# Attention in pairs of heads: the work of two pairs written out as one sequence for each engine, and V split in halves

## The reference

```python
z = einsum('bthd,bshd->bhts', q, k) * HEAD_DIM ** -0.5 + bias
log_beta = log_sigmoid(z)
log_rest = where(k_pos < q_pos, log_sigmoid(-z), 0)
after = cumsum(log_rest, axis=3, reverse=True) - log_rest
a = where(k_pos < q_pos, exp(log_beta + after), 0)
out = einsum('bhts,bshd->bthd', a, v)
```

## Time and profile before

| | us |
|---|---|
| median of 3 runs | 2902.86 (2899.84 to 2904.23) |
| profiled execution | 2905.36, its span 2903.5 |
| attention stage, 1190 to 2010 us of the span | 820.0, PE busy 713.8, DVE 556.1, ACT 494.8 |
| before it, 600 to 1190 | 590.0, PE busy 584.4 |
| after it, 2010 to 2903 | 893.0, PE busy 871.4 |
| granted TensorE clock over the span | 0.960 |

### The profile page before, as it was taken

The page is one execution under the profiler, slowest core; times in us unless marked ns, Lnnn a source line. Parts: engine busy times, 40 slices in busy tenths (PEclk is TensorE's granted clock), DMA queues, the critical chain, the costliest instruction groups (busy, mean ns, idle before and its releaser), DMA issues.

```text
span 2903.5 us, 42452 instructions
## 1 busy us (share of the span) xinstructions
PE 2739.0 (94%) x16785; PEld 2601.4 (90%) x16785; DVE 1328.3 (46%) x1335; ACT 766.3 (26%) x1088; POOL 1007.3 (35%) x534
## 2 busy tenths in 40 slices
PE   7999999999999999989989988977999999999997
PEld 6989999999999999877777777756999999999997
DVE  5243543333333336567657656774343333333335
ACT  5122110000000002556656656663110000000003
POOL 4542476676767761000000000011153343333340
PEclk9999999999999999989989989977999999999998
DMA  3111133333333334222221122223211111111111
GB/s 111 51 31 37 44 116 109 110 109 110 118 113 115 110 113 162 80 72 67 68 76 61 57 78 63 69 80 110 67 58 51 45 44 45 45 51 44 44 37 60
DMA packets 247794, 220.18 MB, mean 76 GB/s; under 512 B 12842, under 2 KB 211298, under 8 KB 247586
## 3 DMA queue, kind: packets, MB, share of 16 engines
q1 hardware_dynamic: 229090, 206.75, 22.7%
q10 hardware_dynamic: 18496, 10.49, 1.2%
HBM read 162.42 MB, written 54.77 MB: 75 GB/s over the span
## 4 chain that ended last, share of the span: by engine, by line
PE 85%; DVE 6%; ACT 4%; issue 3%; ACTq 0%; DMA 0%; SPq 0%; DVEq 0%
PE ps L770 48%; PE ps L899 17%; PE aux L1029 8%; PE ps L936 3%; PE ps L981 2%; PE ps L966 2%; PE ps L954 2%; ACT zb L1312 1%; DVE scratch L1507 1%; PE aux L1000 1%; DVE sp L1637 1%; DVE a_part L1663 1%; PE aux L1035 1%; DVE zb L1670 1%; ACT zb L1323 0%
## 5 line engine op out<-in xcount | busy, mean ns | idle before, releaser
L652 POOL TENSOR_TENSOR w_hi<-w_raw,ones_col 128x1024 fp32r<-128x1024 f32 x140 | 271.0, 1936 | 825.6 <-PE ps L770 540.8
L659 POOL TENSOR_TENSOR w_lo<-w_raw,w_hi 128x1024 fp32r<-128x1024 f32 x156 | 436.1, 2796 | 12.2
L770 PE MATMUL ps<-near_hi,w_hi 128*128 128x352 f32 x1632 | 357.3, 327 | 16.3 <-DVE near_lo L1494 12.9
L770 PE MATMUL ps<-near_lo,w_hi 128*128 128x352 f32 x1632 | 354.2, 325 | 0.0
L770 PE MATMUL ps<-near_hi,w_lo 128*128 128x352 f32 x1632 | 352.5, 324 | 0.0
L726 POOL TENSOR_TENSOR in_lo<-o_back,in_hi 128x1056 fp32r<-128x1056 f32 x7 | 17.2, 2450 | 854.2 <-ACT in_hi L1173 854.2
L770 PEld LDWEIGHTS ps<-near_hi,w_hi 128*128 128x128 f32 x1632 | 278.8, 190 | 20.5 <-issue 11.6
L770 PE MATMUL ps<-in_hi,w_hi 128*128 128x352 f32 x1320 | 286.9, 325 | 3.7 <-issue 3.7
L1621 DVE TENSOR_TENSOR h<-h,ps 128x1056 f32<-128x1056 f32 x160 | 200.2, 1251 | 188.2 <-PE ps L899 188.2
L770 PE MATMUL ps<-in_lo,w_hi 128*128 128x352 f32 x1320 | 285.5, 324 | 0.0
L770 PE MATMUL ps<-in_hi,w_lo 128*128 128x352 f32 x1320 | 284.3, 323 | 0.0
(11 more groups left out here) (229 smaller groups left out, 4457.3 us busy)
## 6 DMA issues: line engine op xcount, KB each, us to landing
w_raw<-in_w_gate_dram SPq DMA_DIRECT2D x44, 512.0 KB, 3.9
w_raw<-in_w_up_dram SPq DMA_DIRECT2D x44, 512.0 KB, 3.9
w_raw<-in_w_down_dram SPq DMA_DIRECT2D x44, 512.0 KB, 3.8
kept_hi<-pre_hi SPq DMA_DIRECT2D x64, 256.0 KB, 2.1
kept_lo<-pre_lo SPq DMA_DIRECT2D x64, 256.0 KB, 2.6
w_hi<-kept_hi SPq DMA_DIRECT2D x32, 512.0 KB, 3.6
w_lo<-kept_lo SPq DMA_DIRECT2D x32, 512.0 KB, 4.5
w_raw<-in_a_w_in_dram SPq DMA_DIRECT2D x16, 512.0 KB, 4.0
```

Of the source, the lines that this page charges most:

```text
L652: gp.tensor_tensor(hi, raw, one, ALU.mult).then_inc(w_hi_done, 1)
L659: gp.tensor_tensor(lo, raw, as32(hi), ALU.subtract).then_inc(w_ready, 1)
L770: last = mm(out[:, c, 0:CH], w[:, ks], x[:, k, c * CH:c * CH + CH], start=(k == 0 and n == 0), stop=(k == KT - 1 and n == 2))
```

## The change

The loop over steps and its tables go. For each of PE, ACT and DVE `pair` now lists every item of a pair by name, in one written order, which begins with what is left over of the pair before (`past`: steps 9 to 11 of it), then the pair's own items (`now`), with the next pair's projections among them (`more`). A last call with `past` alone ends the stage. Items keep their operations and shapes. In detail:

- `softplus_split` becomes `softplus_high` and `softplus_low`, which can be placed apart; the DVE items for the sample are functions of their own, and `q_block` is no longer first in the pair.
- V's split is in two halves of 4 key blocks. `v_high(p, 1)` waits for only the first four `values` of the pair before; `values` of step 4 waits for the other half.
- `chunk_evicted` of Q and V waits for the K or Q split that reads the same part of `staged`.
- SP's and POOL's queues are unchanged.

The diff, cut:

```diff
-X1 = {0: ("c", 0), 1: ("c", 1), 2: ("k", 0), 3: ("c", 2), 4: ("c", 3), 5: ("c", 4), 6: ("c", 5), 7: ("c", 6),
-      8: ("c", 7), 9: ("c", 8), 10: ("v", 1)}
-X2 = {0: ("p", 0), 1: ("p", 1), 2: ("k", 1), 3: ("p", 2), 4: ("k", 2), 5: ("p", 3), 8: ("v", 0), 11: ("v", 2)}
...
                 pe.wait_ge(a_split, NS * p + s + 1)
-                if s == 0:
-                    pe.wait_ge(v_ready, p + 1)
+                if s in (0, TB // P):
+                    pe.wait_ge(v_ready, 2 * p + (1 if s == 0 else 2))
...
-            def pair(p, c, more=True):
-                for s in range(NS + (0 if more else 2)):
-                    if s < NS:
-                        scores(p, c, s)
-                    if s in X1 and (more or X1[s][0] == "p"):
-                        x_turn(p, c, X1[s], more)
-                    at = lagging(p, c, s, 1)
-                    if at is not None:
-                        take_later(*at)
-                    if s == S_OUT:
-                        sample_turned(p, c)
-                    if s in X2 and (more or X2[s][0] == "p"):
-                        x_turn(p, c, X2[s], more)
-                    sample(p, c, s)
-                    if s == S_VALUES:
-                        sample_values(p, c)
-                    for lag, work in ((2, values), (1, carry)):
-                        at = lagging(p, c, s, lag)
-                        if at is not None:
-                            work(*at)
+            def pair(p, c, past=True, now=True, more=True):
+                q, o = p - 1, 1 - c
+                if now:
+                    scores(p, c, 0)
+                if past:
+                    values(q, o, 9)
+                if more:
+                    x_turn(p, c, ("c", 0), more)
+                if past:
+                    carry(q, o, 10)
+                if now:
+                    scores(p, c, 1)
+                    x_turn(p, c, ("p", 0), more)
+                if past:
+                    take_later(q, o, 11)
+                    values(q, o, 10)
+                if more:
+                    x_turn(p, c, ("c", 1), more)
+                if now:
+                    take_later(p, c, 0)
+                if past:
+                    values(q, o, 11)
+                if now:
+                    scores(p, c, 2)
+                    sample_start(p, c)
+                if more:
+                    x_turn(p, c, ("k", 0), more)
+                if now:
+                    carry(p, c, 0)
+                    scores(p, c, 3)
+                    x_turn(p, c, ("p", 1), more)
+                    take_later(p, c, 1)
+                    sample_scores(p, c, 0)
...
+                    x_turn(p, c, ("c", 8), more)
+                if now:
+                    take_later(p, c, 8)
+                    values(p, c, 7)
+                    scores(p, c, 10)
+                    carry(p, c, 8)
+                    sample_later(p, c)
+                    take_later(p, c, 9)
+                    scores(p, c, 11)
+                if more:
+                    x_turn(p, c, ("v", 1), more)
+                if now:
+                    values(p, c, 8)
+                    carry(p, c, 9)
+                    sample_values(p, c)
+                if more:
+                    x_turn(p, c, ("v", 2), more)
+                if now:
+                    take_later(p, c, 10)
+                    sample_turned(p, c)
...
+            pair(PAIRS, 0, now=False, more=False)
...
-            def v_high(p):
+            def v_high(p, half):
+
                 if not isinstance(p, int) or p > 0:
-                    act.wait_ge(pv_done, NS * p)
+                    act.wait_ge(pv_done, NS * p - (NS - 4 if half else 0))
                 act.wait_ge(aux_out, X_ATT + NA * p)
-                nc.scalar.copy(v_part[:, :, 0:4:3, :], v_row[:, 0:RT, :].rearrange("p c (e d) -> p c e d", e=2))\
+                at = slice(RT // 2 * half, RT // 2 * half + RT // 2)
+                nc.scalar.copy(v_part[:, at, 0:4:3, :], v_row[:, at, :].rearrange("p c (e d) -> p c e d", e=2))\
                     .then_inc(v_hi_done, 1)
...
+            def pair(p, c, past=True, now=True, more=True):
+                q, o = p - 1, 1 - c
+                if now:
+                    act.wait_ge(bias_done, p + 1)
+                if past:
+                    weights(q, o, 10)
+                if now:
+                    biased(p, c, 0)
+                    exp_part(p, c, 0)
+                    v_high(p, 1)
+                    log_part(p, c, 0)
+                    turned(p, c, ("p", 0), more)
+                    biased(p, c, 1)
+                if past:
+                    weights(q, o, 11)
...
+                    weights(p, c, 0)
+                    biased(p, c, 2)
+                if more:
+                    turned(p, c, ("k", 0), more)
+                if past:
+                    crossed(q, 0)
+                if now:
+                    turned(p, c, ("p", 1), more)
+                    exp_part(p, c, 2)
...
+                    weights(p, c, 8)
+                    biased(p, c, 10)
+                    crossed(p, 1)
+                    exp_part(p, c, 10)
...
-            def softplus_split(p, c, s):
+            def softplus_high(p, c, s):
                 b, j, c0 = STEPS[s]
-                z = sp[:, s % 2, :, c0:TB]
-                hi, lo = (sp_parts[s % 2][:, x, :, c0:TB] for x in range(2))
-                if s in (0, 1) and (not isinstance(p, int) or p > 0):
+                if s == 0 and (not isinstance(p, int) or p > 0):
+                    dve.wait_ge(carry_done, NCARRY * p)
+                if s == 1 and (not isinstance(p, int) or p > 0):
                     dve.wait_ge(c_done, NS * p)
                 if s >= 2 and s - 2 in CARRY:
                     dve.wait_ge(carry_done, NCARRY * p + CARRY.index(s - 2) + 1)
                 elif s >= 2:
                     dve.wait_ge(c_done, NS * p + s - 1)
                 dve.wait_ge(sp_done, NS * p + s + 1)
-                vec.tensor_copy(hi, z).then_inc(sp_hi_done, 1)
+                vec.tensor_copy(sp_parts[s % 2][:, 0, :, c0:TB], sp[:, s % 2, :, c0:TB]).then_inc(sp_hi_done, 1)
+
+            def softplus_low(p, c, s):
+                b, j, c0 = STEPS[s]
+                hi, lo = (sp_parts[s % 2][:, x, :, c0:TB] for x in range(2))
                 dve.wait_ge(sp_hi_done, NS * p + s + 1)
-                vec.tensor_tensor(lo, z, as32(hi), ALU.subtract).then_inc(sp_split, 1)
+                vec.tensor_tensor(lo, sp[:, s % 2, :, c0:TB], as32(hi), ALU.subtract).then_inc(sp_split, 1)
...
+                if n >= 1:
+                    dve.wait_ge(kq_ready, 6 * (p + 1) + r - NC + 1)
...
+            def v_low(p, half):
+                at = slice(RT // 2 * half, RT // 2 * half + RT // 2)
+                dve.wait_ge(v_hi_done, 2 * p + (1 if half else 2))
+                vec.tensor_tensor(v_part[:, at, 1:3, :], v_row[:, at, :].rearrange("p c (e d) -> p c e d", e=2),
+                                  as32(v_part[:, at, 0:4:3, :]), ALU.subtract).then_inc(v_ready, 1)
...
+            def pair(p, c, past=True, now=True, more=True):
+                q, o = p - 1, 1 - c
+                if past:
+                    logits(q, o, 10)
+                if now:
+                    pair_bias_in(p, c)
+                if past:
+                    softplus(q, o, 11)
+                    softplus_high(q, o, 11)
+                if now:
+                    capped(p, c, 0)
+                if past:
+                    softplus_low(q, o, 11)
+                if more:
+                    chunk_evicted(p, c, 0)
+                if past:
+                    a_low(q, o, 10)
+                if now:
+                    softplus(p, c, 0)
+                if past:
+                    logits(q, o, 11)
+                if now:
+                    capped(p, c, 1)
+                    q_block(p)
+                    softplus_high(p, c, 0)
+                    softplus_low(p, c, 0)
+                if past:
+                    a_low(q, o, 11)
+                if more:
+                    chunk_evicted(p, c, 1)
+                if now:
+                    logits(p, c, 0)
+                    softplus(p, c, 1)
+                    softplus_high(p, c, 1)
+                    softplus_low(p, c, 1)
+                    a_low(p, c, 0)
+                    capped(p, c, 2)
+                    v_low(p, 1)
+                    logits(p, c, 1)
+                if past:
+                    out(q, 0)
+                if now:
+                    softplus(p, c, 2)
...
```

More of the change, by code:

```diff
@@ L130 @@
 CP = (384, 384, 256)
[L133 to L136 removed]
+X_ORDER = [("c", 0), ("p", 0), ("c", 1), ("k", 0), ("p", 1), ("k", 1), ("c", 2), ("p", 2), ("c", 3), ("k", 2),
+           ("c", 4), ("p", 3), ("c", 5), ("c", 6), ("c", 7), ("v", 0), ("c", 8), ("v", 1), ("v", 2)]
 AUX_ORDER = [item for item in X_ORDER if item[0] != "c"]
 NA = len(AUX_ORDER)
[L139 to L145 removed]
 def aux_at(p, item, more=True):
@@ new lines, in sample_start @@
```

(39 more changed lines are left out.)

359 lines of the change are left out of this document (253 added, 106 removed).

## The result

The changed kernel takes 2781.05 us (median of 4 runs, 2778.8 to 2783.0) against 2902.01 for the kernel before (4 runs): a ratio of 0.9583, 95% interval 0.9566 to 0.9599. The forecast was 2829 with a range of 2792 to 2878.

A forecast was written before the change was run, and what follows sets the result against it. PE bounds the kernel, losing time to late neighbours and a low clock; a pair was 83.4 + 2.4 + 2.5 + 3.4 = 91.7 us. Over all stretches -73.9 from 2905.4, so 2829 on the median (2810 to 2855; 8 in 10: 2792 to 2878).

The forecast's parts named there:

- the floor of a pair: PE work in the 101.14 us stretch at 2.4 GHz: less 9.6 idle and 8.1 for the clock, 83.4 us.
- the clock: Time still lost at 1.2 GHz in each pair: +3.4 us, some 40% of the present loss, bounds 0 and 8.1.
- the waits: PE's waits left in a pair: 1.4 + 1.0 us, and 2.5 for about a dozen short ones of 0.2.
- two stretches without projections: Light PE work left in each pair: about 10 us (steps 1 to 3, sample) and 13 us (steps 9 to 11, sample's end).
- The late start of a pair: At a pair's start, ACT's leftover work delays DVE's first-chunk eviction to 8.5 us; PE, ready at 7.1, newly waits 1.4.
- a dozen handovers: Places in a pair where PE arrives together with its input: about a dozen of 0.2 us, 2.5 us in all.
- The jump: Loop's back jump in two stretches, 6.2 us over their neighbours: 4 left, so 96 us each, -22.8 together.
- The lap that I gave as its limit: Last pair, full step: logarithm, softplus, copy, split, weight split, cap, two exponentials, 7.3 us; full steps gain little, whole pair -10.
- One sign: Granted clock of the attention stage should rise from 0.88 to about 0.93.
- A: Rival: the clock holds and the last pair reaches its bound, 34 us further, 2795 (up to 2810); chance 0.20.
- Waits move: Rival: PE's waits move instead of going, half the gain, 40 us less, 2863 (2855 to 2897); chance 0.23.
- slower: Rival: clock stays at 1.2 GHz through both stretches of each pair lacking projections, 2963 us; chance 0.07.

The follow-up runs named there:

- the trial with the gap put back: Changed kernel with values 8 moved right behind take_later 9, ahead of scores 11 and the V turn on PE: 2806.0 us, ratio 0.9669.
- the repeated sample round: Changed kernel with the first round of sample scores (8 matmuls of 8 columns) made ten times over in each pair, no wait added: 2903.1 us, ratio 1.0004.
- kernel without the loop: Changed kernel with pairs 1 to 6 written out on PE, ACT and DVE instead of a hardware loop of three passes: 2770.6 us, ratio 0.9549.
- moving the caps: Changed kernel with pairs 1 to 6 written out, caps of steps 6 and 7 ahead of the splits in the last pair: 2770.9 us, ratio 0.9547.
- the turns together: Changed kernel with K turn, page turn and second K turn in a row behind the sample start, both sample rounds adjacent: 2833.9 us, ratio 0.9770.

## Why the prediction was right and wrong

- **What bounds the kernel: right.** PE was the resource, its waits were those on neighbours late in their own queue, and the floor of a pair, 83.4 us by idle and clock, was met: 82.86 us of PE busy in 83.74. DVE and ACT kept out of the way with 69.1 and 61.6 us.
- **Two terms of the sum failed: the clock, 3.4 us a pair for 0, and the waits, 4.9 for 0.9.** They are 3.4 and 4.0 of the 8.0 us between my 91.7 and the measured 83.74; the other 0.5 is the floor, 83.4 for 82.86.
- **The clock.** I put +3.4 us a pair on it and kept two stretches without projections as a reason. Measured: 0, the clock is 1.00 in every pair without a jump, but for the one into the last pair (0.94). One of my two reasons was a misreading. I took the window of 10 us around the idle of 3.44 us, at 0.94, as a sign that a gap doesn't bring the clock down. That window ends just behind the fall. By single microseconds of the kernel before, PE starting again at 1368.57:

```profile
1366.00:1367.00 1.00, 0.00 (x0) 0.00 (x0) 0.00 (x0) 0.99 (x2) 0.00 (x0) 1.00 0.22 64
1368.00:1369.00 1.00, 0.43 (x3) 0.46 (x4) 0.97 (x2) 0.13 (x1) 0.00 (x0) 0.88 0.13 38
1371.00:1372.00 1.00, 1.00 (x7) 0.35 (x4) 0.67 (x1) 0.00 (x0) 0.00 (x0) 0.50 0.23 66
```

  So closing that gap gave its clock back too, as the trial with the gap put back shows in reverse. This was the smaller part, some 3 of the 20 us that this pair ran at 1.2 GHz. The larger part began at 1290 us, behind the page turn and the sample start, and went on over two waits (1.90 and 0.87 us) to 1307; how much of it each of them is to blame for isn't shown. The other reason, that light work brings the clock down with hardly any idle (0.26 us at the page turn), is true; the repeated sample round shows it. What I didn't do is ask how light the new order is. In the kernel before, the page turn, the sample start and a sample round stand in one run; in the new order a carry and scores stand between the sample start and the page turn. That this is what keeps the clock at 1.00 there is likely, but no run changes it alone. The estimate "40% of the present loss" came from nothing but caution.
- **The waits: sized too large, 4.9 us for 0.9.** The late start of a pair was to cost 1.4 us; PE waited 0.16 for the eviction. Most of this is a slip in adding: copies of 0.9, issues of 1.58 and two operations of 1.06, begun 1.5 us ahead of the pair, end 3.1 us into it and not "about 4". Measured, ACT ends them 2.9 us after PE's first scores of the pair (1517.58), and the eviction ends 6.9 after, where I had 8.5. ACT in the changed kernel at the end of a pair:

```profile
1517.31 0.39 ACTq L1462 DMA_DIRECT2D out_dram<-v_row  x1
1517.79 0.54 ACTq L1463 DMA_DIRECT2D out_dram<-v_row  x1
1518.37 1.06 ACT L1410 ACTIVATE sp<-sp 128x1024 f32<-128x1024 f32 x1 [1.09 <-issue]
```

  The two V row issues took 0.39 and 0.54 us, where I had taken 0.41 and 1.17 from one pair. Across the pairs of the kernel before the second one varies from 0.54 to 2.03 us; across seven pairs of the changed one it is 0.54 to 0.60. At step 8 I had 1.0 and it is 0.73, as the row with the idle time shows:

```profile
1513.63 0.63 PE L973 MATMUL ps<-a_part,v_part 128*128 128x128 f32 x4 [0.73 <-DVE scratch L1894]
...
1524.67 0.65 PE L1027 MATMUL aux<-ident,k_page 128*128 128x128 f32 x4 [0.16 <-DVE staged L1869]
```

  Those two waits are the whole idle time of a pair (0.89 us), so nothing is left of the 2.5 us for "a dozen handovers". My reading is that they are already in the durations of the rows, which reach some 0.1 us into the next instruction (DVE's split of the softplus at 1522.84 takes 1.22 us, and the next one starts 1.13 behind it); no run was made for it.
- **The jump: too small.** I left 4 us of the 6.2; the stretches with it are 89.2 and 89.85, 5.5 and 6.1 over. PE's own wait there is as before, 3.19 us where it was 2.98:

```profile
1431.60 0.90 PE L928 MATMUL ps<-kq 64*128 64x128 f32 x6 [3.19 <-issue]
```

  The kernel without the loop gave 10.4 us for two of them.
- **By the terms of the sum:** the three stretches without the jump gave 52.9 us for 28.1, the two with it 35.8 for 22.8, the first 12.6 for 7, the one into the last pair 11.0 for 6, the last pair 10.8 for 10, and the rest of the span lost 0.9.
- **The last pair: right in size**, and the output waits that I named for it are gone (7.2 us, now 0.3). The lap that I gave as its limit is not confirmed: moving the caps did nothing. Its sum was wrong as well, since the items named, with the logarithm, make 8.4 us and not 7.3; and DVE's durations in it are those of the last section.
- **One sign misleads:** the clock of the whole stage was to be about 0.93, and it is 0.94. It is made of 1.00 in the pairs, 0.96 in the two with the jump, 0.94 in the one into the last pair and 0.70 in the last, and not of the small loss in each pair that I had in mind.
- **V in halves at no cost: right** (1.0001). **The rivals**: A, the clock holds, was the nearest at 2795, and it had 0.20 to the forecast's 0.45. It still left the waits of 4.9 us in place, and so stayed above the measured time. "Waits move" and "slower" are real, but for other kernels: mixing the orders of two designs gave 1.010 and 1.013.
- The rule of the Trainium skill ("TensorE: Matmul & The Clock Gate", "Why this matters for your kernels") on idle gaps would have given the clock's part in full, and the trace after agrees with it: 0.9 us of idle and 1.00. The repeated sample round, 0.53 with 0 idle, shows that it isn't the whole of it.

## What to carry to other kernels

When holes of 1 to 3 us among short matmuls are closed, take the clock as part of the gain: price PE's idle and its time at 1.2 GHz in the stretch as two terms, and give back both unless the new order runs more light work in one piece than any stretch of the old trace that kept 2.4 GHz. (That is my rule from these runs; it was not tried on another kernel.) Read the clock around a gap in windows of 1 us: in one of 10 us the fall right behind it can hide. An order over several in-order queues is one thing: half of it can be slower than none. When following an order by hand, add durations or handovers, not both, add the chain up a second time, and take a DMA issue's price from more than one pair.

## What the runs showed that I had not expected

One gap of 2.2 us in a pair cost three times its idle by way of the clock (1.45 us of idle, 3.05 of slower matmuls). With the turns together, 2.3 us more of idle came with 6.2 of slower matmuls.

In the last pair DVE instructions are held up while POOL works. The timeline of POOL and DVE in the changed kernel:

```profile
1820.98 2.48 POOL L718 TENSOR_TENSOR in_lo<-o_back,in_hi 128x1056 fp32r<-128x1056 f32 x1 [6.31 <-ACT in_hi L1254]
...
1821.67 2.87 DVE L1822 TENSOR_TENSOR sp<-zb,sp 128x1024 f32<-128x1024 f32 x1
...
1831.56 2.51 POOL L718 TENSOR_TENSOR in_lo<-o_back,in_hi 128x1056 fp32r<-128x1056 f32 x1 [8.11 <-ACT in_hi L1254]
1831.88 2.75 DVE L1835 CAST sp_part<-sp 128x1024 fp32r<-128x1024 f32 x1
```

The softplus takes 2.87 us and ends 1.1 us after POOL's subtraction; the cast takes 2.75. In the seven stretches before, where POOL is idle, the same softplus takes 1.22 on average:

```profile
L1822 DVE TENSOR_TENSOR sp<-zb,sp 128x1024 f32<-128x1024 f32 x42 | 51.1, 1217 | 7.1 <-ACT sp L1416 7.1
```

With the subtractions on DVE (line 1818 is the softplus, 1831 the cast) no DVE instruction of the last pair is stretched. Two of its groups, a softplus of 128x768 and a cast:

```profile
L1818 DVE TENSOR_TENSOR sp<-zb,sp 128x768 f32<-128x768 f32 x2 | 1.9, 958 | 0.1
...
L1831 DVE CAST sp_part<-sp 128x1024 fp32r<-128x1024 f32 x2 | 1.4, 694 | 0.2
```

while the kernel without the loop, the one to compare with, has the same two groups stretched (lines 1820 and 1833). There the hold falls on the softplus of 128x768 and not on that of 128x1024 (1.22): it depends on what DVE starts while POOL works.

```profile
L1820 DVE TENSOR_TENSOR sp<-zb,sp 128x768 f32<-128x768 f32 x2 | 4.2, 2077 | 0.1
...
L1833 DVE CAST sp_part<-sp 128x1024 fp32r<-128x1024 f32 x2 | 3.5, 1725 | 0.2
```

The Trainium skill ("SBUF — State Buffer", "SBUF: two separate sides") says that DVE, when it reads two inputs from SBUF (against a GpSimd instruction that reads SBUF) or runs in a 2-port mode, shares a port pair with GpSimd under a lock that the first to start holds for its whole instruction. The runs agree: two-input softplus, cast and cap (2.19 us for 0.29) are held up. The logits, which read one input from PSUM, are not: one that starts 0.35 us into a subtraction takes 1.23 us as elsewhere. My 1.35 us for the softplus was a mean over both kinds: in the kernel before, at 128x1024, it takes 1.21 us in the stretches ahead of the last pair and 2.17 in the last.
